# Linear attention of a two-block network: the next head's preparation in nine pieces in place of seven

## The chip, the cores and the metric

The kernel runs on one core of a Trainium2 chip. The metric is the device time of one execution, in microseconds (us); lower is better.

## The reference, cut to what matters

The program is a small network: two layers with four mixers each, then a block with gated linear attention, then a mixture of experts. Only the linear attention matters here. It has 4 heads; the keys of a head have 128 dimensions, its values 256. It runs over 512 tokens and 256 context tokens in chunks of 64, forwards and backwards:

```python
def step(s, inp):                      # one chunk of 64 tokens
    qc, kc, vc, gc = inp
    cum = jnp.cumsum(gc, axis=2)
    last = cum[:, :, -1:, :]
    s_new = jnp.exp(last[:, :, 0, :])[..., None] * s + jnp.einsum(
        'bhjd,bhje->bhde', kc * jnp.exp(last - cum), vc)
    ...
    scores = jnp.einsum('bhid,bhjd,bhijd->bhij', qc, kc, decay)
    o = jnp.einsum('bhid,bhde->bhie', qc * jnp.exp(cum), s) + jnp.einsum(
        'bhij,bhje->bhie', scores, vc)
    return s_new, o
```

where `gc` is `log_sigmoid` of the gates, divided by 16. So each head needs the running sums of its log gates within each chunk, their exponentials on keys and queries, and then a chain of states from chunk to chunk.

## The kernel before, in words

The stage is `gla_heads`. For each head there are two streams of work, written as Python generators, one for each engine: `gla_prepare_stream` makes a head's operands, `gla_scan_stream` uses them. A `yield` ends a piece. `run` takes a plan, a list of stream numbers, and issues the next piece of the named stream on each engine. All engines follow the same plan, each with its own pieces, so the plan and the places of the `yield`s are each engine's program order. An engine works strictly in that order; semaphores hold it where data or a buffer is missing.

The plan first lists the whole preparation of head 0. Then, for heads 0 to 2, it mixes the 17 pieces of the scan of head h with the pieces of the preparation of head h+1 by `alternate(17, steps)`, which puts a piece in as soon as its share of the scan's pieces is done. The last head is scanned with no preparation beside it. A third stream (modulation, L1687 and L1694) puts one piece behind the first of each scan.

**The scan's 17 pieces.** Scores (L2816 on TensorE, masked by VectorE at L2896, and the first pair of update matmuls); values (L2833); then twelve steps s0 to s11, s0 to s3 over the context and s4 to s11 over the tokens. In step s TensorE makes the pair of update matmuls for step s+1 (L2803, one for each direction, into banks that alternate), and from s4 on multiplies the state of step s-1 into the output (L2849). VectorE adds the update to the decayed state (L2910, a pair; L2907 in s0). It may not overwrite a state buffer until the product that reads it is done. Three closing pieces: ScalarE squares the output (L2874); TensorE sums over a head (L2859) and ScalarE makes the root (L2877, L2879); VectorE reads the output out (L2918, L2919).

**The preparation's pieces.** TensorE makes the gates for z = 0 and z = 1, one direction each (L2554); ScalarE takes them (L2563, L2565) and makes the softplus (L2571, L2573). VectorE waits for it and makes the minimum (L2578) and three running sums (L2580), then the centring: totals, halves, two subtractions, an addition and a clamp (L2588 to L2594). Each of these waits for the one ahead of it. The values are turned (L2639) and copied (L2692, L2697). ScalarE makes the exponentials (L2598 to L2603) from the clamped sums, VectorE scales keys and queries with them (L2611, L2615, L2620, L2622), and last the keys are turned and copied (L2714).

The first head's gates are prepared in the projection stage ahead (`gla_project`), in the shadow of its matmuls, by the same helpers.

Of the kernel before, what the change touches and what calls it, by code (L numbers as in the profile page):

```python
# [28 lines left out]
ALU = mybir.AluOpType  # L29
AXX = mybir.AxisListType.X  # L30

P = 128
# [9 lines left out]
CH = 64  # L42
# [2235 lines left out]
class Gla:  # L2278
# [3 lines left out]
    LAT, SEG = S, S + CTX  # L2282
# [38 lines left out]
def gla_project(c, w, gates, ahead, sums, first_sums, swept):  # L2321
# [23 lines left out]
    with nc.Block() as block:  # L2345
# [140 lines left out]
        @block.vector  # L2486
        def _(dve):
            eng = nc.vector
            apply.dve(dve)
            dve.wait_ge(ctx["summed"], 1)  # L2490
            eng.tensor_tensor(c.ctxmod[:, :], c.ps[:, 7, 0:2 * KT], c.ctxmod[:, :], ALU.add).then_inc(ctx["ready"], 1)
            dve.wait_ge(ctx["ready"], 1)
            eng.tensor_scalar(ctx_gain, ctx_scale, 1.0, None, ALU.add).then_inc(ctx["ready"], 1)
            dve.wait_ge(ctx["ready"], 2)
            eng.tensor_tensor(ctx_gain, ctx_gain, c.cols2[:, C2_AT["norm1_g"]:C2_AT["norm1_g"] + KT], ALU.mult
                              ).then_inc(ctx["ready"], 1)
            dve.wait_ge(ctx["ready"], 3)

            def low(t):
                dve.wait_ge(ctx["high"], t + 1)  # L2500
                eng.scalar_tensor_tensor(c.ctx_lo[:, t, :], w.ctx_h[:, t, :], ctx_shift[:, t:t + 1],
                                         c.ctx_hi[:, t, :].bitcast(F32), ALU.add, ALU.subtract).then_inc(ctx["low"], 1)

            for t in range(n1):
                if t + 2 < n1:
                    qr.split_low(dve, (t + 2) % RING, (t + 2) // RING)
                if t == 5:
                    dve.wait_ge(ctx["rooted"], 2)
                if 5 <= t < 9:
                    for kt in range(2 * t - 10, 2 * t - 8):  # L2510
                        eng.scalar_tensor_tensor(w.ctx_h[:, kt, :], w.ctx_x[:, kt, :], ctx_gain[:, kt:kt + 1], ctx_rs,
                                                 ALU.mult, ALU.mult).then_inc(ctx["scaled"], 1)
                        if kt:
                            low(kt - 1)
                if t == 9:
                    low(KT - 1)
                    dve.wait_ge(low_split, 1)
                    eng.tensor_tensor(low_lo[:, :], low_w, low_hi[:, :].bitcast(F32), ALU.subtract).then_inc(low_split, 1)
                for n in early(t):
                    sums.add(dve, n)  # L2520

            def copy_ctx(s, g):
                dve.wait_ge(kv.multiplied, g * RING + s + 1)
                t = g * RING + s
                eng.tensor_copy(ctx_kv[:, t * CTX:(t + 1) * CTX], c.ps[:, RING + t % 2, 0:CTX]).then_inc(ctx_emptied, 1)
                if t < FIRST_GATE:
                    for n in late(t):
                        sums.add(dve, n)
                elif t == FIRST_GATE + 2:
                    gates.scan(dve, 0)  # L2530
                elif t == FIRST_GATE + 3:
                    gates.centre(0)
                elif t == FIRST_GATE + 5:
                    gates.scale(dve, 0)

            kv.split_first(dve, kv.split_low)
            kv.tiles(dve, kv.split_low, copy_ctx)


class GlaGates:  # L2540
# [31 lines left out]
        act.wait_ge(self.pr["exp"], h + 1)  # L2572
        self.c.nc.scalar.activation(cum, cum, ACT.Ln, bias=1.0).then_inc(self.pr["soft"], 1)  # L2573

    def scan(self, dve, h):
        eng, g, cum = self.c.nc.vector, self.w.g[h], self.w.cum[h]
        dve.wait_ge(self.pr["soft"], h + 1)
        self.chain(eng.scalar_tensor_tensor(g, g, 0.0, cum, ALU.min, ALU.subtract))  # L2578
        for i in range(3):
            self.chain(eng.tensor_tensor_scan(cum[:, i * S:(i + 1) * S], self.c.const("scan"), g[:, i * S:(i + 1) * S], 0.0,  # L2580
                                              ALU.mult, ALU.add))

    def centre(self, h):
        eng, w, g, cum, chain = self.c.nc.vector, self.w, self.w.g[h], self.w.cum[h], self.chain
        SEG = w.SEG
        chunks = lambda t: t.rearrange("p (c n) -> p c n", n=CH)
        bc = lambda t, n: t.unsqueeze(2).to_broadcast([P, n, CH])
        chain(eng.tensor_copy(w.tot, chunks(cum)[:, :, CH - 1]))  # L2588
        chain(eng.tensor_scalar(w.half, w.tot, 0.5, None, ALU.mult))
        f, r = cum[:, 0:SEG], cum[:, SEG:2 * SEG]  # L2590
        chain(eng.tensor_tensor(chunks(f), chunks(f), bc(w.half[:, 0:12], 12), ALU.subtract))
        chain(eng.tensor_tensor(r, g[:, SEG:2 * SEG], r, ALU.subtract))
        chain(eng.tensor_tensor(chunks(r), chunks(r), bc(w.half[:, 12:24], 12), ALU.add))
        eng.tensor_scalar(cum, cum, 80.0 * 16, -80.0 * 16, ALU.min, ALU.max).then_inc(self.pr["gate"], 1)  # L2594
# [31 lines left out]
def gla_prepare_stream(c, w, gates, pr, sn, copied):  # L2626
# [7 lines left out]
    def pe():  # L2634
        eng = nc.tensor

        def turn(bank, blocks):
            for n, x in enumerate(blocks):
                last = eng.transpose(bank[:, n * P:(n + 1) * P], x, c.const("ident"))  # L2639
            return last  # L2640

        for h in range(GLA_H):
            if h:
                eng.wait_ge(pr["k_out"], 6 * h)
                eng.wait_ge(copied, h)
                if h == 1:
                    eng.wait_ge(pr["v_out"], 4)
                gates.gate(eng, h, 0, A, B)
            yield
            if h:  # L2650
                eng.wait_ge(pr["z_in"], 8 * h + 4)
                gates.gate(eng, h, 1, A, B)
            yield
            if h:
                eng.wait_ge(pr["z_in"], 8 * h + 8)
            for j in range(2):
                v = c.p[:, w.v + 2 * h + j, :]
                turn(v_banks(h)[j], [v[:, n * P:(n + 1) * P] for n in range(4)]).then_inc(pr["v_turn"], 1)
            yield
            if h:  # L2660
                eng.wait_ge(pr["v_out"], 4 * h + 1)
            turn(v_banks(h)[2], [w.vc[:, 2 * h + j, n * P:(n + 1) * P] for j in range(2) for n in range(2)]
                 ).then_inc(pr["v_turn"], 1)
            yield
            yield
            yield
            if h:
                eng.wait_ge(pr["v_out"], 4 * h + 4)
            for i in range(3):
                eng.wait_ge(pr["k_done"], 4 * h + (1, 3, 4)[i])  # L2670
                if h and i == 2:
                    eng.wait_ge(pr["k_out"], 6 * h + 2)
                turn(k_banks(h)[i], [w.e_neg[:, n * P:(n + 1) * P] for n in range(4 * i, 4 * i + 4)]
                     ).then_inc(pr["k_turn"], 1)
            yield

    def act():
        eng, on = nc.scalar, nc.scalar.activation
        for h in range(GLA_H):
# [10 lines left out]
            for j in range(2):  # L2690
                eng.wait_ge(pr["v_turn"], 3 * h + j + 1)
                on(w.v_tok[q][:, 0:4, j * P:(j + 1) * P], v_banks(h)[j].rearrange("p (b n) -> p b n", n=P), ACT.Copy  # L2692
                   ).then_inc(pr["v_out"], 1)
            yield
            eng.wait_ge(pr["v_turn"], 3 * h + 3)
            for j in range(2):
                on(w.v_tok[q][:, 4:6, j * P:(j + 1) * P],  # L2697
                   v_banks(h)[2][:, 2 * j * P:2 * (j + 1) * P].rearrange("p (b n) -> p b n", n=P), ACT.Copy
                   ).then_inc(pr["v_out"], 1)
            yield  # L2700
            if h:
                eng.wait_ge(pr["gate"], h + 1)
# [14 lines left out]
    def dve():  # L2717
        eng = nc.vector
        for h in range(GLA_H):
            yield  # L2720
            yield
            if h:
                gates.scan(eng, h)
            yield
            if h:
                gates.centre(h)
            yield
            yield
            if h:
                gates.scale(eng, h, (lambda: eng.wait_ge(sn["e_scaled"], 2 * (h - 1))) if h >= 2 else None)  # L2730
            yield
            yield

    return dict(pe=pe, act=act, dve=dve, steps=7)


def gla_scan_stream(c, w, pr, sn, fill, filled, w_out):
# [245 lines left out]
def gla_heads(c, w, gates, pr, sums, fill, filled, w_out, swept):  # L2983
# [3 lines left out]
                                            "ms", "rs", "ended")}  # L2987
    mod = ModRows(c, "b2_mod", sums, lambda j: sums.sums[0][1][j][:, 0:S], lambda j: c.ps[:, 0, :], c.ps[:, 0, :])
    prep = gla_prepare_stream(c, w, gates, pr, sn, mod.copied)
    scan = gla_scan_stream(c, w, pr, sn, fill, filled, w_out)  # L2990

# [19 lines left out]
    modulation = dict(pe=sum_parts, dve=add_bias, act=copy_parts)  # L3011
    opened = open_gla_stream(c, w, gates, pr, sn, w_out, [(pr["k_out"], 6 * GLA_H), (sums.biased, 1), (mod.copied, sums.count)])
    streams = [scan, prep, modulation, opened]
    plan = [1] * prep["steps"]
    for h in range(GLA_H - 1):
# [893 lines left out]
```

## Time and profile before

| | us |
|---|---|
| median of 3 runs | 2521.93 (2519.75 to 2528.81) |
| the profiled execution, its own time | 2520.24 |
| its span | 2518.2 |
| TensorE busy | 2269.8 (90%) |
| VectorE busy | 1589.3 (63%) |
| ScalarE busy | 1075.6 (43%) |
| mean granted TensorE clock | 0.965 of full |

The span is the time from the first to the last instruction of the profiled execution; its own time has some 2 us more around it. Busy times are of the whole program. The stage `gla_heads` begins near 1927 us of the span and ends near 2092 us.

### The profile page before, as it was taken

The numbers are of one execution on the slowest core, as the hardware profiler recorded it, in microseconds if no ns is written. First come the engines' busy times: TensorE is split into PE (matmuls) and PEld (weight loads), VectorE is DVE, ScalarE is ACT, GpSimd is POOL, SyncE is SP. The second block draws the span as 40 slices with busy tenths as digits, with TensorE's granted clock in tenths as the row PEclk, the third lists the DMA queues.
The fourth block names the chain that finished last, engine by engine and source line by source line (L and its number), as shares of the span: only waits on it lengthen the run. The fifth ranks groups of instructions, "written<-read, shape, count | busy, mean of one in ns | idle before, by whom it ended". The sixth has DMA issues, their size and how long they took to land. (4 is left out here: it accounts for less than half of the span.)

```text
span 2518.2 us, 31929 instructions
## 1 busy us (share of the span) xinstructions
PE 2269.8 (90%) x11349; PEld 1814.9 (72%) x11349; DVE 1589.3 (63%) x2284; ACT 1075.6 (43%) x1628; POOL 123.3 (5%) x201
## 2 busy tenths in 40 slices
PE   4998689899999989877889999999999888699995
PEld 3776567678888867666667888788877676588884
DVE  6655656555567665665665555774633774699997
ACT  3343244443343235342343333423233443588884
POOL 0001100000000000110000000000000000011112
PEclk9999899999999999999999999998999999799997
DMA  7650000223225355200012223354633101699996
GB/s 293 210 185 9 1 34 1 83 77 97 94 76 210 118 178 201 65 1 1 35 43 81 95 92 103 137 172 162 223 109 134 34 1 43 264 401 412 413 411 233
DMA packets 95430, 348.29 MB, mean 138 GB/s; under 512 B 12360, under 2 KB 14520, under 8 KB 95056
## 3 DMA queue, kind: packets, MB, share of 16 engines
q1 hardware_dynamic: 88688, 323.67, 36.0%
q0 software_dynamic: 3888, 14.16, 1.5%
q10 hardware_dynamic: 2736, 8.92, 0.9%
q8 instruction: 70, 1.15, 0.2%
q14 instruction: 48, 0.39, 0.1%
HBM read 333.55 MB, written 21.54 MB: 141 GB/s over the span
## 5 line engine op out<-in xcount | busy, mean ns | idle before, releaser
L500 PE MATMUL ps<-a_hi,w_hi 128*128 128x512 f32 x1344 | 545.6, 406 | 28.8 <-DVE h_lo L406 18.1
L502 PE MATMUL ps<-a_hi,w_lo 128*128 128x512 f32 x1344 | 538.2, 400 | 0.0
L501 PE MATMUL ps<-h_lo,w_hi 128*128 128x512 f32 x1280 | 508.8, 398 | 0.0
L464 DVE TENSOR_TENSOR w_lo<-ring,w_hi 128x1024 fp32r<-128x1024 f32 x178 | 218.2, 1226 | 378.0 <-ACT w_hi L459 377.5
L459 ACT ACTIVATE w_hi<-ring 128x1024 fp32r<-128x1024 f32 x178 | 187.9, 1058 | 512.5 <-PE ps L502 507.1
L500 PEld LDWEIGHTS ps<-a_hi,w_hi 128*128 128x128 f32 x1344 | 255.9, 190 | 98.5 <-issue 26.8
L502 PEld LDWEIGHTS ps<-a_hi,w_lo 128*128 128x128 f32 x1344 | 255.8, 190 | 63.2
L501 PEld LDWEIGHTS ps<-h_lo,w_hi 128*128 128x128 f32 x1280 | 243.4, 190 | 60.7 <-issue 2.9
L3362 DVE TENSOR_TENSOR moe_w_lo<-p,moe_w_hi 128x1024 fp32r<-128x1024 f32 x204 | 240.2, 1222 | 8.0 <-ACT moe_w_hi L3461 2.0
L3461 ACT ACTIVATE moe_w_hi<-p 128x1024 fp32r<-128x1024 f32 x204 | 216.1, 1063 | 56.8 <-PE ps L3404 53.9
L2139 PE MATMUL ps<-p_lo,down_hi 128*128 128x512 f32 x352 | 138.0, 392 | 0.0
L3402 PE MATMUL ps<-moe_w_hi,moe_x_hi 128*128 128x512 f32 x272 | 108.9, 401 | 6.4 <-DVE moe_w_lo L3362 6.4
L3404 PE MATMUL ps<-moe_w_lo,moe_x_hi 128*128 128x512 f32 x272 | 107.2, 394 | 0.0
L3403 PE MATMUL ps<-moe_w_hi,moe_x_lo 128*128 128x512 f32 x272 | 106.9, 393 | 0.0
L2056 ACT ACTIVATE down_hi<-down_raw 128x1408 fp32r<-128x1408 f32 x32 | 44.2, 1380 | 144.7 <-PE ps L2140 144.7
L501 PE MATMUL ps<-y_lo,w_hi 128*128 128x512 f32 x192 | 76.6, 399 | 0.0
L2139 PEld LDWEIGHTS ps<-p_lo,down_hi 128*128 128x128 f32 x352 | 66.1, 188 | 14.3
L291 DVE SCALAR_TENSOR_TENSOR y<-vt,cond,y 128x1024 f32<-128x1024 f32 x56 | 70.7, 1280 | 5.7 <-DMA vt<-in_ada 5.7
L2060 DVE TENSOR_TENSOR down_lo<-down_raw,down_hi 128x1408 fp32r<-128x1408 f32 x32 | 52.0, 1625 | 33.7 <-ACT down_hi L2056 33.4
L1991 DVE SCALAR_TENSOR_TENSOR y<-ps,cols,y 128x510 f32<-128x510 f32 x88 | 65.9, 749 | 11.0 <-DVE y L1988 0.5
L1961 ACT ACTIVATE y<-ps,cols 128x512 f32<-128x512 f32 x88 | 67.3, 764 | 9.4 <-PE ps L502 9.4
L1988 DVE SCALAR_TENSOR_TENSOR y<-ps,cols,y 128x511 f32<-128x511 f32 x88 | 65.6, 746 | 4.6 <-ACT y L1961 4.6
(645 smaller groups left out, 4200.3 us busy)
## 6 DMA issues: line engine op xcount, KB each, us to landing
ring<-in_ffn_up SPq DMA_DIRECT2D x88, 512.0 KB, 3.4
ring<-in_w_in SPq DMA_DIRECT2D x72, 512.0 KB, 5.3
p<-in_moe_gate SPq DMA_DIRECT2D x68, 512.0 KB, 7.4
p<-in_moe_up SPq DMA_DIRECT2D x68, 512.0 KB, 7.4
p<-in_moe_down SPq DMA_DIRECT2D x68, 512.0 KB, 8.4
vt<-in_ada SPq DMA_DIRECT2D x64, 512.0 KB, 4.0
p<-in_ada SPq DMA_DIRECT2D x48, 512.0 KB, 5.4
down_raw<-in_ffn_down SPq DMA_DIRECT2D x32, 704.0 KB, 5.0
```

The source lines that it names most:

```text
L291: ins = nc.vector.scalar_tensor_tensor(out, self.piece[b], factor, out, ALU.mult, ALU.add)
L459: self.c.nc.scalar.activation(self.c.w_hi[:, s % 2, :], self.c.slot(s), ACT.Copy).then_inc(self.high, 1)
L464: self.c.nc.vector.tensor_tensor(self.c.w_lo[:, s % 2, :], self.c.slot(s), self.c.w_hi[:, s % 2, :].bitcast(F32), ALU.subtract).then_inc(s ...
L500: nc.tensor.matmul(bank, c.w_hi[:, s % 2, at], hi(kt), start=(kt == self.order[0]), stop=False)
L501: nc.tensor.matmul(bank, c.w_hi[:, s % 2, at], lo(kt), start=False, stop=False)
L502: return nc.tensor.matmul(bank, c.w_lo[:, s % 2, at], hi(kt), start=False, stop=(kt == self.order[-1]))
L2139: nc.tensor.matmul(bank, down.w_hi[n % 2][:, at], c.p_lo[:, kt, :], start=False, stop=False)
L3362: ops.tensor_tensor(m.w_lo[:, n % 4, :], m.raw[n], m.w_hi[:, n % 4, :].bitcast(F32), ALU.subtract).then_inc(low[n], 1)
L3402: nc.tensor.matmul(bank, x[0], w_hi, start=start, stop=False)
L3403: nc.tensor.matmul(bank, x[1], w_hi, start=False, stop=False)
L3404: return nc.tensor.matmul(bank, x[0], w_lo, start=False, stop=stop)
L3461: nc.scalar.activation(m.w_hi[:, n % 4, :], m.raw[n], ACT.Copy).then_inc(high[n], 1)
```

## The change

The preparation has nine pieces in place of seven, in each engine's generator. VectorE's running sums are cut in two pieces, one with the minimum and the first sum, one with the other two, and its centring likewise, after the forward subtraction. TensorE's and ScalarE's generators get two empty pieces each, so that their pieces keep their partners. By the larger number of pieces `alternate` also places all of them anew. In the projection the two halves of the centring are called one behind the other.

```diff
-    def scan(self, dve, h):
+    def running(self, dve, h, parts=(0, 1, 2)):
         eng, g, cum = self.c.nc.vector, self.w.g[h], self.w.cum[h]
-        dve.wait_ge(self.pr["soft"], h + 1)
-        self.chain(eng.scalar_tensor_tensor(g, g, 0.0, cum, ALU.min, ALU.subtract))
-        for i in range(3):
+        if 0 in parts:
+            dve.wait_ge(self.pr["soft"], h + 1)
+            self.chain(eng.scalar_tensor_tensor(g, g, 0.0, cum, ALU.min, ALU.subtract))
+        for i in parts:
             self.chain(eng.tensor_tensor_scan(...))
...
-    def centre(self, h):
+    def centre_first(self, h):
...
-        f, r = cum[:, 0:SEG], cum[:, SEG:2 * SEG]
+        f = cum[:, 0:SEG]
         chain(eng.tensor_tensor(chunks(f), chunks(f), bc(w.half[:, 0:12], 12), ALU.subtract))
+
+    def centre_second(self, h):
...
+        r = cum[:, SEG:2 * SEG]
         chain(eng.tensor_tensor(r, g[:, SEG:2 * SEG], r, ALU.subtract))
         chain(eng.tensor_tensor(chunks(r), chunks(r), bc(w.half[:, 12:24], 12), ALU.add))
         eng.tensor_scalar(cum, cum, 80.0 * 16, -80.0 * 16, ALU.min, ALU.max).then_inc(self.pr["gate"], 1)
...
@@ def pe():
             yield
+            yield
             if h:
                 eng.wait_ge(pr["v_out"], 4 * h + 1)
             turn(v_banks(h)[2], ...)
             yield
+            yield
...
@@ def act():
+            yield
             eng.wait_ge(pr["v_turn"], 3 * h + 3)
...
             yield
+            yield
             if h:
                 eng.wait_ge(pr["gate"], h + 1)
...
@@ def dve():
             if h:
-                gates.scan(eng, h)
+                gates.running(eng, h, (0,))
             yield
             if h:
-                gates.centre(h)
+                gates.running(eng, h, (1, 2))
+            yield
+            if h:
+                gates.centre_first(h)
+            yield
+            if h:
+                gates.centre_second(h)
             yield
...
-    return dict(pe=pe, act=act, dve=dve, steps=7)
+    return dict(pe=pe, act=act, dve=dve, steps=9)
```

## Rows read from the trace of the kernel before

**Rows 1.** The page, part 1: busy time, share of the span, instructions, by engine.

```profile
PE 2269.8 (90%) x11349; PEld 1814.9 (72%) x11349; DVE 1589.3 (63%) x2284; ACT 1075.6 (43%) x1628; POOL 123.3 (5%) x201
```

**Rows 2.** Timeline, VectorE, head 1's period: start, length, instruction, idle before.

```profile
...
1994.52 1.76 DVE L2578 SCALAR_TENSOR_TENSOR h<-h 128x1536 f32<-128x1536 f32 x1 [1.32 <-ACT h L2573]
1996.31 3.74 DVE L2580 TENSOR_TENSOR_SCAN h<-k,h 128x512 f32<-128x512 f32 x3
2000.09 1.66 DVE L2910 SCALAR_TENSOR_TENSOR h<-h,small,ps 128x256 f32<-128x256 f32 x4
2001.66 0.18 DVE L2588 COPY small<-h 128x24 f32<-128x24 f32 x1
...
2003.08 0.96 DVE L2592 TENSOR_TENSOR h<-h 128x768 f32<-128x768 f32 x1
...
2008.64 0.93 DVE L2910 SCALAR_TENSOR_TENSOR h<-h,small,ps 128x256 f32<-128x256 f32 x2 [0.83 <-PE ps L2849]
...
2014.95 0.75 DVE L2918 SCALAR_TENSOR_TENSOR w2b<-ps,cols,w2b 128x512 f32<-128x512 f32 x1 [2.07 <-ACT w2b L2879]
...
```

**Rows 3.** Timeline, TensorE, the same period.

```profile
...
1983.94 0.60 PE L2803 MATMUL ps<-w2b,p 128*128 128x256 f32 x2
...
1984.90 1.55 PE L2554 MATMUL ps<-vt,ring 16*128 16x512 f32 x4
...
1991.62 1.00 PE L2849 MATMUL ps<-w2b,h 128*128 128x64 f32 x8
1992.46 0.65 PE L2803 MATMUL ps<-w2b 128*128 128x256 f32 x2
...
1994.21 1.04 PE L2639 MATMUL ps<-k,p 128*128 128x128 f32 x8
...
2000.63 1.22 PE L2803 MATMUL ps<-w2b 128*128 128x256 f32 x2 [3.67 <-DVE h L2910]
...
2007.99 2.79 PE L2849 MATMUL ps<-w2b,h 128*128 128x64 f32 x24
...
```

**Rows 4.** Timeline, ScalarE, the same period.

```profile
...
1986.06 0.69 ACT L2563 ACTIVATE h<-ps,cols 128x512 f32<-128x512 f32 x1 [5.08 <-PE ps L2554]
...
1987.57 0.48 ACT L2565 ACTIVATE h<-ps,cols 128x256 f32<-128x256 f32 x1
...
2006.06 1.48 ACT L2598 ACTIVATE ring<-h 128x1536 f32<-128x1536 f32 x1 [0.21 <-DVE h L2594]
2007.45 1.13 ACT L2602 ACTIVATE ring<-h 128x512 f32<-128x512 f32 x2
2008.49 0.21 ACT L2603 ACTIVATE small<-small 128x24 f32<-128x24 f32 x1
2010.82 1.08 ACT L2874 ACTIVATE w2b<-ps 128x512 f32<-128x512 f32 x2 [2.12 <-PE ps L2849]
...
```

**Rows 5.** Timeline, VectorE's minimum and ScalarE's squares, heads 0 and 2.

```profile
...
1954.56 1.76 DVE L2578 SCALAR_TENSOR_TENSOR h<-h 128x1536 f32<-128x1536 f32 x1 [1.33 <-ACT h L2573]
...
1970.30 1.08 ACT L2874 ACTIVATE ring<-ps 128x512 f32<-128x512 f32 x2 [1.56 <-PE ps L2849]
...
2034.78 1.76 DVE L2578 SCALAR_TENSOR_TENSOR h<-h 128x1536 f32<-128x1536 f32 x1 [1.33 <-ACT h L2573]
...
2051.42 1.08 ACT L2874 ACTIVATE ring<-ps 128x512 f32<-128x512 f32 x2 [2.46 <-PE ps L2849]
...
```

**Rows 6.** Windows of 7 us behind TensorE's idle stretch, three heads.

```profile
core 0: us, PE busy (x) PEld busy (x) DVE busy (x) ACT busy (x) POOL busy (x), PEclk, DMA share, GB/s
1960.66:1967.66 7.00, 6.91 (x35) 6.24 (x35) 6.80 (x13) 2.22 (x4) 0.00 (x0) 0.76 0.00 1
2000.63:2007.63 7.00, 7.00 (x31) 6.37 (x32) 6.75 (x13) 2.23 (x4) 0.00 (x0) 0.63 0.00 0
2040.89:2047.89 7.00, 7.00 (x29) 6.35 (x30) 6.06 (x12) 2.22 (x4) 0.00 (x0) 0.58 0.00 0
```

**Rows 7.** Timeline, SyncE's DMA issues: the first load of expert weights.

```profile
...
2166.08 2.10 SPq L3376 DMA_DIRECT2D p<-in_moe_gate  x4
...
```

More of the change, by code:

```diff
@@ L2529, in copy_ctx @@
                 elif t == FIRST_GATE + 2:
-                    gates.scan(dve, 0)
+                    gates.running(dve, 0)
                 elif t == FIRST_GATE + 3:
-                    gates.centre(0)
+                    gates.centre_first(0)
+                    gates.centre_second(0)
                 elif t == FIRST_GATE + 5:
@@ L2589, in centre @@
         chain(eng.tensor_scalar(w.half, w.tot, 0.5, None, ALU.mult))
-        f, r = cum[:, 0:SEG], cum[:, SEG:2 * SEG]
+        f = cum[:, 0:SEG]
         chain(eng.tensor_tensor(chunks(f), chunks(f), bc(w.half[:, 0:12], 12), ALU.subtract))
+    def centre_second(self, h):
+        eng, w, g, cum, chain = self.c.nc.vector, self.w, self.w.g[h], self.w.cum[h], self.chain
+        SEG = w.SEG
+        chunks = lambda t: t.rearrange("p (c n) -> p c n", n=CH)
+        bc = lambda t, n: t.unsqueeze(2).to_broadcast([P, n, CH])
+        r = cum[:, SEG:2 * SEG]
         chain(eng.tensor_tensor(r, g[:, SEG:2 * SEG], r, ALU.subtract))
```

## The prediction

> **What bounds the kernel now.** I read the page first. TensorE is busy nearly throughout, but that is an average over stages, and the diff touches only three head periods of the linear attention [rows 1]. So I went to the timeline of one such period, head 1's scan with the preparation of head 2, engine by engine: VectorE [rows 2], TensorE [rows 3], ScalarE [rows 4]. In what follows s0 to s11 are the steps of the scan; each has an update on VectorE (pair of L2910), a pair of matmuls on TensorE that makes the next update (L2803), and from s4 on the products that add the state to the output (L2849). A pair has two halves, one for each direction.
>
> The period runs so. After the values (L2833) TensorE goes s0, gate z0 (L2554), s1, s2, gate z1, s3 and so on [rows 3]. ScalarE takes the gates and makes the softplus; VectorE waits for its end and starts the gate chain at 1994.52 [rows 2]. I call that moment X. The minimum (L2578) and three running sums (L2580) then hold VectorE without a break to 2000.09, and TensorE, which had run ahead, stands idle 3.67 us until s6's first half is there [rows 2, 3]. Then s6 and s7, all of the centring, s8, s9, and s10 at 2008.64. From 2000.63 TensorE works without a pause up to its last product, and the squares (L2874) start at 2010.82, just behind it [rows 3, 4]. So the end of the period is set by the softplus, 5.6 us of VectorE, and then TensorE's backlog. The exponentials (L2598 to L2603) began at 2006.06 and were done before the squares' data was: they cost nothing [rows 4]. Behind the squares the order is the same in both kernels: mean, root, readout at 2014.95 [rows 2], next head.
>
> What I count is therefore the distance from X to the squares. It is 15.74 us in head 0, 16.30 in head 1 and 16.64 in head 2 (from the start of L2578 to that of L2874; the other two heads are in [rows 5]). The three differ because TensorE's granted clock fell after the idle stretch: over the 7 us behind it the mean was 0.76, 0.63 and 0.58, with 0.5 the lower level, 1.2 GHz [rows 6]. Lost work time is 7 us by the missing share: 1.7, 2.6 and 2.9 us, together 7.2.
>
> **The change part by part.** Writing out the two plans (17 scan steps against 7 or 9 pieces, each piece put where its share of the scan is done):
>
> before: s0, G0, s1 s2, G1, s3 s4 s5, [minimum, 3 sums], s6 s7, [all centring], s8 s9 s10, exponentials;
> after: G0, s0 s1, G1, s2 s3, [minimum, sum 1], s4 s5, [sums 2 and 3], s6 s7, [centring, first], s8 s9, [centring, second], s10 s11, exponentials.
>
> The turn of the context values stays behind s7, scaling stays between s10 and the readout, the key turns stay last. No instruction, copy or DMA is added, and SP's and GpSimd's queues are not passed. In the projection the same instructions run in the same order, and for head 0 nothing runs beside the nine pieces: both cost 0.
>
> *The gates, one step earlier.* G1 now has one pair fewer ahead of it, and a pair takes 0.96 us (1983.94 to 1984.90) [rows 3]. The take of z0 begins 1.16 us behind G0 and lasts 2.0 us (1986.06 to 1988.05 [rows 4]), so it is out 3.15 us after G0's start. G1 must wait for that, and comes behind G0's 1.55 us and two pairs, 3.4 us after G0: no wait. X comes 0.93 us sooner. The updates s1 to s3 wait for the gates instead, but this is ahead of X: they are done 3 us before it.
>
> *VectorE behind X.* Minimum 1.79 us (to the next start), each sum 1.26, two steps together 1.57 (2000.09 to 2001.66), first centring 1.42 (2001.66 to 2003.08), second 2.94 to the clamp's end (2003.08 [rows 2] to the exponentials' start at 2006.06 [rows 4], less 0.04 from an end to what waits for it). Before, VectorE sat 1.3 us ahead of the minimum and had done s4 and s5 by then. Now it will sit some 3 us there, since s4 and s5 stand behind the minimum in its program: the split does not fill the wait, it lengthens it.
>
> *TensorE behind X.* Products of a step 0.84 us (1991.62 to 1992.46), the four context turns 0.44 (half of the eight value turns' 1.04, less the 0.16 by which the last matmul overlaps what follows, as in the products' row) [rows 3]. s4 starts at X+3.05, and TensorE resumes 0.54 behind it as it did at 2000.63: X+3.59. What it has ahead of the idle stretch is all it had before less two pairs and two products (3.6 us), so it falls idle near 1993.5 and resumes near 1997.2, for 3.7 us: the stretch moves and keeps its length. Then pair 6, products 5, pair 7, products 6: 3.6 us, X+7.2. Pair 8 needs s6, which starts at X+3.05+1.57+2.52 = X+7.14, hence X+7.68. Pair 8, products 7, turn, pair 9: 0.96+0.84+0.44+0.96 = 3.2, so products 8 start at X+10.88. s9 may not overwrite the state that products 8 read; before, s10 started 0.65 behind the products it waits for (2007.99 to 2008.64), so s9 starts at X+11.53 and lasts 0.87. VectorE alone would have been there at X+10.4 or so.
>
> *Centring, second, and the exponentials.* Clamp's end X+11.53+0.87+2.94 = X+15.34, exponentials 0.04 later. From their start to the next activation I take 2.54 us: 2006.06 to 2008.70, less the 0.1 by which an activation here starts ahead of its predecessor's end (2008.58 against 2008.49) [rows 4], and the squares stand behind them in ScalarE's program: X+17.92. s10 and products 11 are done by X+17, so the exponentials, formerly free, set the end. The scaling moves back too (to the end of its first exponential), but the readout's 2.07 us of waiting [rows 2] covers most of it and it moves with the squares.
>
> *Sum.* At full clock: 17.92-0.93 = 16.99 against 15.74, 16.30, 16.64: +1.25, +0.69, +0.35, together +2.3 us. If the clock falls as before, the loss L comes in ahead of products 8 and replaces the 0.48 us that pair 8 waited: 17.44+L-0.93, thus 18.21, 19.11, 19.41, or +2.5, +2.8, +2.8, together +8.1. The idle stretch that brought the fall has the same length (3.7 against 3.67), so I go near the upper case, with one stretch in some five getting off: **+7 us**. The last head has no preparation and moves along. Nothing absorbs it later: the first expert weights are asked for at 2166.08, behind the routing, and that comes from this stage's output [rows 7].
>
> The page Perfetto Trace Analysis of the Trainium skill, section Optimizing Scalar/DVE Operations, says that where VectorE and ScalarE are not saturated but cause bubbles on another engine, breaking up instructions may let work finish sooner. It speaks for this change; by it the bubbles would shrink, which is the first rival below.
>
> **Rivals.** *The idle stretch goes (faster).* VectorE's block of 5.6 us is cut to 3.05, 2.52, 1.42 and 2.94; if TensorE's idle time and the fall of the clock went with it, 3 x 3.67 + 7.2 = 18.2 us would go: 2521.9-18.2 = 2504. It decides if TensorE has work for more than X+3.59 in front of it. Against it: it has 3.6 us less in hand. A smaller form: if only the exponentials were clear of the squares, the squares would follow s10 (X+14.56+0.91+0.8-0.93 = 15.3), -0.4, -1.0, -1.3: -2.7, 2519. Against it: program order. Chance of a gain in either form 0.10, above 0.5% 0.02.
>
> *Nothing (the pieces hide).* If products 8 do not hold s9 and clock stays high, the clamp ends at X+14.64 and the squares start at X+17.22-0.93 = 16.3: +0.2 in all, 2522. For it: the margin that holds s9 is only about 1 us at full clock. With the full-clock case of +2.3 (2524): 0.25.
>
> *A second fall of the clock (slower still).* TensorE would have two more gaps in each head, about 1.4 us ahead of products 11 and 1.7 ahead of the mean. If the clock falls there, mean and score products run at half speed on the path: as much again as behind the first gap, 1.7 to 2.9 us a head, +7: 2536. The page TensorE: Matmul & The Clock Gate of the Trainium skill, Part 1, has it that the throttled clock is the resting state and activity lifts it; the trace agrees as far as [rows 6] go. Before, gaps of this size behind the squares (0.69 and 1.76 us) left the clock at full. Chance 0.10.
>
> **How the numbers follow.** Forecast +7: 0.55. Profiled execution 2520.2 us (span 2518.2) would become 2527; the median of the three runs is 1.7 above it, so 2521.9+7 = 2529. Range: from the hidden case less a little, 2520, to the second fall, 2536; this leaves out the large gain and ends beyond +14. A measurement of this kernel can't tell a change within 0.5%, 12.6 us, from none. Only the full gain (0.02) is faster by more; slower by more takes the second fall and more (0.06); the rest, 0.92, is within.
>
> **What the profile would show.** L2578 0.9 us earlier within each period, with some 3 us of idle VectorE ahead of it; TensorE's idle stretch still near 3.7 us but between products 4 and pair 6; an idle stretch of VectorE ahead of s9 released by L2849; the squares released by ScalarE's own exponentials, not by L2849, 17.9 to 20.3 us behind L2578; period 42 to 43 us in place of 40. I am wrong if pieces 4 and 5 leave TensorE no idle stretch, if s9 starts right behind s8, or if the clock behind the gap stays at full in all three heads.

## The result, and the profile after

The changed kernel takes 2536.6 us (median of 6 runs, 2533.6 to 2538.8) against 2521.3 (6 runs, 2519.8 to 2528.8): ratio 1.0058, 95% interval 1.0048 to 1.0068. That is 15.3 us more, where the forecast was 7 us more (2528.8), the range ended at 2536, and slower by more than 0.5% had a chance of 0.06. The direction was right, the size half.

VectorE in head 1's period, from the timeline of the changed kernel (start, length, instruction, idle before). It answers to [rows 2]; L2580 is the minimum, L2582 the sums, L2929 the updates, L2590 to L2603 the centring, L2937 the readout.

```profile
1998.27 1.76 DVE L2580 SCALAR_TENSOR_TENSOR h<-h 128x1536 f32<-128x1536 f32 x1 [3.08 <-ACT h L2574]
2000.07 1.23 DVE L2582 TENSOR_TENSOR_SCAN h<-k,h 128x512 f32<-128x512 f32 x1
2001.33 1.66 DVE L2929 SCALAR_TENSOR_TENSOR h<-h,small,ps 128x256 f32<-128x256 f32 x4
...
2007.64 0.93 DVE L2929 SCALAR_TENSOR_TENSOR h<-h,small,ps 128x256 f32<-128x256 f32 x2 [1.35 <-PE ps L2868]
...
2011.54 0.93 DVE L2929 SCALAR_TENSOR_TENSOR h<-h,small,ps 128x256 f32<-128x256 f32 x2 [0.77 <-PE ps L2868]
...
2014.37 0.96 DVE L2603 TENSOR_SCALAR h<-h 128x1536 f32<-128x1536 f32 x1
2015.24 0.87 DVE L2929 SCALAR_TENSOR_TENSOR h<-h,small,ps 128x256 f32<-128x256 f32 x2
...
2023.81 0.75 DVE L2937 SCALAR_TENSOR_TENSOR w2b<-ps,cols,w2b 128x512 f32<-128x512 f32 x1 [3.54 <-ACT w2b L2898]
```

TensorE in the same period, answering to [rows 3]; L2822 are the pairs, L2868 the products, L2878 the mean.

```profile
2001.87 1.22 PE L2822 MATMUL ps<-w2b 128*128 128x256 f32 x2 [3.76 <-DVE h L2929]
...
2010.89 1.00 PE L2868 MATMUL ps<-w2b,h 128*128 128x64 f32 x8
...
2012.65 1.89 PE L2868 MATMUL ps<-w2b,h 128*128 128x64 f32 x16
2015.77 1.10 PE L2868 MATMUL ps<-w2b,h 128*128 128x64 f32 x8 [1.23 <-DVE h L2929]
2018.53 3.78 PE L2878 MATMUL ps<-w2b,k 128*128 128x512 f32 x4 [1.65 <-ACT w2b L2893]
```

ScalarE, answering to [rows 4]: the exponentials (L2607 to L2612) and the squares (L2893).

```profile
2015.36 1.48 ACT L2607 ACTIVATE ring<-h 128x1536 f32<-128x1536 f32 x1 [4.47 <-DVE h L2603]
2016.75 1.13 ACT L2611 ACTIVATE ring<-h 128x512 f32<-128x512 f32 x2
2017.79 0.21 ACT L2612 ACTIVATE small<-small 128x24 f32<-128x24 f32 x1
2017.90 1.06 ACT L2893 ACTIVATE w2b<-ps 128x512 f32<-128x512 f32 x2
2022.35 0.69 ACT L2896 ACTIVATE w2b<-ps,k 128x512 f32<-128x512 f32 x1 [3.38 <-PE ps L2878]
```

The reader is to see three things. VectorE waits 3.08 us for the softplus, then 1.35 and 0.77 us for products of TensorE. The squares start 0.11 us behind the exponentials' last start, and have no wait on TensorE of their own: they are held by ScalarE's program order. And the mean, 1.98 us before, takes 3.78.

The last is the clock. Windows of 7 us in the changed kernel, first behind the first gap in each head (answering to [rows 6]), then around the mean:

```profile
core 0: us, PE busy (x) PEld busy (x) DVE busy (x) ACT busy (x) POOL busy (x), PEclk, DMA share, GB/s
1958.11:1965.11 7.00, 7.00 (x37) 6.39 (x38) 6.25 (x12) 0.00 (x0) 0.00 (x0) 0.76 0.00 0
2001.87:2008.87 7.00, 7.00 (x30) 6.24 (x31) 5.54 (x11) 0.00 (x0) 0.00 (x0) 0.65 0.00 0
2046.36:2053.36 7.00, 7.00 (x31) 6.25 (x31) 5.57 (x12) 0.00 (x0) 0.00 (x0) 0.65 0.01 2
1973.00:1980.00 7.00, 5.49 (x12) 2.91 (x12) 3.11 (x10) 3.56 (x8) 3.11 (x6) 0.53 0.00 0
2017.50:2024.50 7.00, 5.49 (x12) 2.91 (x12) 3.46 (x10) 3.56 (x8) 0.00 (x0) 0.54 0.00 0
2062.00:2069.00 7.00, 5.31 (x12) 2.90 (x12) 3.46 (x10) 3.56 (x9) 0.00 (x0) 0.55 0.00 0
```

The same stretch around the mean in the kernel before, head 1:

```profile
2010.50:2017.50 7.00, 4.56 (x47) 3.04 (x48) 4.83 (x12) 4.96 (x9) 0.00 (x0) 1.00 0.01 2
```

Behind the first gap the clock falls as it did before (0.76, 0.65, 0.65 against 0.76, 0.63, 0.58 in [rows 6]). Around the mean it is at the lower level, 1.2 GHz, in all three heads, where before it was at full.

Two measures serve all that follows. The first is the stage's length, from the copy of s0 in head 0 (L2907, now L2926) to the squares of the last head: 2081.36-1937.09 = 144.3 us before, 2094.34-1937.73 = 156.6 after, +12.3. What lies outside it differs by 3.8 us between the two profiled executions; among all the executions profiled below, the way from the last squares to the first load of expert weights took 84.1 to 86.4 us and the rest 352.0 to 354.6, whatever the change, so I do not count that as the change's. The stage itself began (copy of s0 in head 0) between 1934.4 and 1938.4 us in all of them but two. In runs 10 and 11 it began at 1946.7 and 1945.4: their profiled executions, 2528.9 and 2541.5 us, were the slowest of their runs, and what made them so lies for the most part ahead of the stage. Each version's stage is read from one execution. The second measure is the distance from the minimum's start to the squares and to the readout in heads 0, 1, 2.

### The profile page after: what moved, and what is told of

The parts are those of the page before. It is cut to its first block and busy times, and to the rows that moved or that the text cites. A ratio compares the mean times of both kernels' runs of the same rounds, so it can differ in the third digit from the quotient of the medians.

```text
span 2534.3 us, 31932 instructions
## 1 busy us (share of the span) xinstructions
PE 2282.2 (90%) x11349; PEld 1820.7 (72%) x11349; DVE 1588.2 (63%) x2284; ACT 1074.7 (42%) x1628; POOL 124.3 (5%) x201
```

## The experiments

All twelve runs use the changed kernel's nine pieces with a plan written out: `places` gives for each piece the scan piece (0 to 16; s0 is 2, s11 is 13) behind which it stands. The new places are 1, 3, 5, 7, 9, 11, 13, 15, 16; the old, in the same pieces, 2, 4, 7, 7, 9, 9, 12, 14, 16. The pieces in order: gate z0, gate z1, minimum with first sum, other sums, first half of the centring (and the context values), second half, exponentials, scaling, key turns.

```diff
+    places = [...]
     plan = [1] * prep["steps"]
     for h in range(GLA_H - 1):
-        steps = alternate(scan["steps"], prep["steps"])
-        at = steps.index(0) + 1
-        plan += steps[:at] + [2] + steps[at:]
+        for i in range(scan["steps"]):
+            plan += [0] + [2] * (i == 0) + [1] * places.count(i)
```

| run | median us | ratio, 95% | stage us | squares behind minimum | mean |
|---|---|---|---|---|---|
| before | 2521.3 | | 144.3 | 15.74, 16.30, 16.64 | 1.98, 1.99, 1.98 |
| changed | 2536.6 | 1.0048 to 1.0068 | 156.6 | 18.88, 19.63, 19.86 | 3.78, 3.78, 3.78 |
| 1 old places | 2520.5 | 0.9992 to 1.0009 | 144.2 | 15.74, 16.28, 16.63 | 1.98, 1.98, 1.98 |
| 2 gates early | 2520.2 | 0.9985 to 1.0003 | 142.8 | 15.73, 16.99, 15.75 | 1.98, 1.98, 1.98 |
| 3 sums split | 2531.7 | 1.0028 to 1.0054 | 155.2 | 18.06, 18.83, 19.60 | 1.98, 1.98, 3.66 |
| 4 centring split | 2534.7 | 1.0035 to 1.0061 | 157.0 | 17.88, 18.87, 19.05 | 3.78, 3.78, 3.78 |
| 5 exponentials behind | 2533.1 | 1.0045 to 1.0074 | 157.4 | 17.89, 19.04, 19.62 | 3.78, 3.63, 3.63 |
| 6 later gaps filled | 2531.6 | 1.0028 to 1.0054 | 154.6 | 19.50, 19.71, 20.77 | 1.98, 1.98, 1.98 |
| 7 all gaps filled | 2523.4 | 1.0006 to 1.0025 | 147.8 | 17.80, 17.80, 18.09 | 1.98, 1.98, 1.98 |
| 8 old, gap filled | 2524.2 | 1.0006 to 1.0024 | 147.4 | 15.74, 15.74, 18.07 | 1.98, 1.98, 3.78 |
| 9 s10 ahead | 2534.3 | 1.0030 to 1.0062 | 158.9 | 17.09, 17.71, 17.84 | 1.98, 1.98, 1.98 |
| 10 s8 between | 2518.3 | 0.9978 to 0.9996 | 142.7 | 16.55, 17.07, 15.45 | 1.98, 1.98, 1.98 |
| 11 gap at product filled | 2532.3 | 1.0025 to 1.0057 | 155.7 | 18.89, 21.36, 19.18 | 1.98, 3.46, 2.81 |
| 12 gap at mean filled | 2533.6 | 1.0032 to 1.0066 | 158.0 | 18.88, 19.79, 21.93 | 2.39, 2.77, 2.93 |

The last column is the length of the mean's four matmuls in the timeline of the profiled execution. Ratios are against runs of the kernel before on the same chip, whose medians were 2520.6 to 2521.5.

### 1: the pieces at the old places

```diff
+    places = [2, 4, 7, 7, 9, 9, 12, 14, 16]
```

> The changed kernel's nine pieces, each put where the same work stood in the seven-piece plan. Theory (places alone matter): every engine's order is that of before, so 2521 us, 0 within 3 us. Rival (the pieces themselves, more yields and calls, cost something): up to the full +15 us, 2536.

2520.5 us; the three distances are those of before to 0.02 us. More pieces cost nothing. The whole change is where they stand.

### 2: only the gates early

```diff
+    places = [1, 3, 7, 7, 9, 9, 12, 14, 16]
```

> Only the two gate pieces at the new places, all else at the old. Theory: the softplus ends 0.93 us sooner in each of three heads, VectorE's block and TensorE's resumption with it, the idle stretch shrinks from 3.67 to about 2.7 us: -2.8 us, 2518.4, and up to 4 us less if the granted clock then holds (2514). Rival (updates s1 to s3 come late behind the gates and delay the period): +1 to +3 us.

VectorE's wait for the softplus is 0.47 us in place of 1.32, TensorE's idle stretch 2.80 in place of 3.67: the 0.87 us is there (0.93 was reckoned). The stage is 1.5 us shorter, the median 1.1 us lower, and the interval of the ratio includes 1. The distance was 15.73 and 15.75 us in heads 0 and 2, a floor that run 8 explains, and 16.99 in head 1. And in head 0 the clock, which held behind the first gap, fell a little later, in front of head 1's scores (0.57 of full over the 4 us from 1976.68), behind a wait of TensorE of 2.02 us for the copies of the turned keys (L2727); before, 2.01 us of the same wait left it at full. So the gain is of the right kind and half the size, and too small to be shown by the runs alone.

### 3 and 4: one split each

```diff
+    places = [2, 4, 5, 7, 9, 9, 12, 14, 16]     # 3: sums split
+    places = [2, 4, 7, 7, 9, 11, 12, 14, 16]    # 4: centring split
```

> Only the running sums cut in two, with s4 and s5 between them, all else at the old places; the centring stays whole between s7 and s8. Theory: TensorE's idle stretch grows to about 4.7 us and pair 10 waits for s8 behind the centring; squares 17.2 to 17.9 us behind the minimum in place of 15.7 to 16.6: +3 to +5 us, 2524 to 2526. Rival (the sums' split is harmless, the centring's is all of it): 0.

> Only the centring cut in two, with s8 and s9 between, all else at the old places. Theory: s9 waits for products 8, so the second half and the exponentials come late and hold the squares: 16.4 us behind the minimum plus the clock's loss of 1.7 to 2.9, +7 us, 2529; with a second fall of the clock ahead of the mean (2.1 us a head more) 2535. Rival (squares still follow TensorE, exponentials are hidden): 0.

Each alone costs nearly all: +10.9 us of the stage for the sums, +12.7 for the centring; together, with the gates early, +12.3. They don't add, and they hold the period in different places. In 3 the squares never stood behind the exponentials: they waited 1.57 us for TensorE, and TensorE had waited 1.39 us ahead of pair 10 for s8, which stood behind the whole centring (head 1). In 4 the timeline of VectorE and of ScalarE shows the two holders that the prediction names, in head 1:

```profile
2011.48 0.93 DVE L2929 SCALAR_TENSOR_TENSOR h<-h,small,ps 128x256 f32<-128x256 f32 x2 [2.16 <-PE ps L2868]
...
2014.30 0.96 DVE L2603 TENSOR_SCALAR h<-h 128x1536 f32<-128x1536 f32 x1
```

```profile
2015.30 1.48 ACT L2607 ACTIVATE ring<-h 128x1536 f32<-128x1536 f32 x1 [5.00 <-DVE h L2603]
...
2017.84 1.06 ACT L2893 ACTIVATE w2b<-ps 128x512 f32<-128x512 f32 x2
```

s9 waits 2.16 us for products 8, and the second half of the centring, the clamp and the exponentials stand behind it. I had 16.4 us and the clock's loss of 1.7 to 2.9, so 18.1 to 19.3; it was 17.9 to 19.1. The second fall of the clock came in all three heads and made it the 2535 of the expectation. For 3 I had named +3 to +5 and it was +10.9: s7 waited for products 6 (1.37 us in head 1) ahead of the whole centring, which I had left out there, and the clock fell again in head 2's mean and in front of head 1's scores (0.57 over the 4 us from 1980.22).

### 5: the exponentials behind the squares

```diff
+    places = [1, 3, 5, 7, 9, 11, 14, 15, 16]
```

> The changed kernel with one piece moved: the exponentials stand behind the squares in ScalarE's order instead of ahead of them. Theory (exponentials hold the squares and open the gap in which the clock falls a second time): squares some 1.5 us closer to the minimum, mean at full clock, but the scaling now waits for the exponentials and holds the readout; 2 us a head back, 2530. Rival (TensorE's backlog holds the squares): 2536 or more, as the root comes later behind 2.5 us of exponentials.

ScalarE's timeline, head 1:

```profile
2016.30 1.09 ACT L2893 ACTIVATE w2b<-ps 128x512 f32<-128x512 f32 x2 [6.03 <-PE ps L2868]
2017.27 1.48 ACT L2607 ACTIVATE ring<-h 128x1536 f32<-128x1536 f32 x1
```

The squares now wait for TensorE (6.03 us), 1.0, 0.6 and 0.2 us sooner behind the minimum than in the changed kernel. So the exponentials' hold on the squares is real and small. The mean still took 3.63 us and more, though the gap ahead of it had shrunk from 1.65 to 0.69 us: my view that the exponentials open the gap in which the clock falls does not stand by itself. The 1.23 us gap ahead of the last product, which the second half of the centring makes by standing in front of s10, was still there. In head 0 the keys' copies then came late, TensorE waited 3.21 us for them, and the clock fell once more in front of head 1's scores. 2533.1 us lies between the two numbers, and the stage, 157.4, is no shorter than the changed kernel's.

### 6, 7 and 8: gaps filled with matmuls that nothing reads

```diff
+        def warm(n, bank=None):
+            for _ in range(n):
+                eng.matmul(c.ps[:, 7 if bank is None else bank, 2 * P:4 * P], c.const("ones"), c.k[:, 0:2 * P], start=True, stop=True)
...
+                    if s == STEPS - 1 and z == 0 and h < GLA_H - 1:   # 6 and 7, ahead of the last product
+                        warm(2)
...
+            if h < GLA_H - 1:                                        # 6 and 7, ahead of the mean
+                warm(3)
...
+                if s == 5 and h < GLA_H - 1:                         # 7; in 8: s == 7, warm(7, 1), old places
+                    eng.wait_ge(pr["v_out"], 4 * (h + 1) + 2)
+                    warm(5, 1)
```

> The changed kernel with idle-time matmuls that nothing reads, two ahead of the last product and three ahead of the mean in heads 0 to 2 (128x256 each, 0.48 us), so that TensorE's second and third gap are filled. Theory (the second fall of the clock costs 2.1 us a head): mean at 1.98 us instead of 3.78, -6 us against the changed kernel, 2530. Rival (the fall comes from elsewhere, or filling delays the work): 2536 or more.

> As the one before, and five such matmuls also in the first gap, ahead of pair 6. Theory: with no fall of the clock at all the changed order costs what the prediction's full-clock sum says, squares 17.9 us behind the minimum: 2521 + 2.3 + 0.5, near 2524. Rival (waits between VectorE and TensorE cost more than the clock): 2528 or more.

In 6 the mean is back at 1.98 us in all heads and the readout stands 4.1 to 4.5 us behind the squares, where it was 5.9 to 6.3; the median is 5.0 us lower than the changed kernel's. But the stage is only 2.0 us shorter, though the readouts give back 5.4: the squares came 1.6 us later in all, and in head 0 TensorE now waited 2.35 us for the keys' copies in place of 0.92 and the clock fell there instead, at 1978.1, so that head 1's minimum stood 1.4 us further behind the readout.

In 7 the clock holds at full behind the first gap and around the mean in all three heads. Windows of the run, behind the first gap and around the mean in heads 0 to 2:

```profile
1953.00:1960.00 7.00, 6.47 (x40) 5.43 (x39) 6.85 (x13) 0.00 (x0) 0.00 (x0) 1.00 0.05 19
1968.50:1975.50 7.00, 4.35 (x33) 2.57 (x33) 4.80 (x12) 4.82 (x10) 3.11 (x6) 1.00 0.00 1
2011.00:2018.00 7.00, 4.94 (x50) 3.07 (x49) 5.16 (x12) 5.28 (x11) 0.00 (x0) 1.00 0.00 0
2052.00:2059.00 7.00, 4.95 (x50) 3.15 (x49) 5.16 (x12) 5.28 (x11) 0.00 (x0) 1.00 0.01 2
```

It still fell once, as in run 6 in front of head 1's scores, behind the same 2.35 us:

```profile
1974.52 0.63 PE L2648 MATMUL ps<-k,ring 128*128 128x128 f32 x4 [2.35 <-ACT p L2727]
```

```profile
1976.00:1978.00 2.00, 1.79 (x17) 1.42 (x14) 1.19 (x4) 0.81 (x2) 1.14 (x2) 0.50 0.00 0
```

The squares come 17.80, 17.80 and 18.09 us behind the minimum: the prediction's full-clock chain gave 17.92. The stage is 3.5 us longer than before (2.3 by that chain; 1.2 is the longer way from head 0's readout to head 1's minimum, where the clock fell), the median 2523.4. So filling all three gaps takes 8.8 us off the stage's +12.3. That is not quite the clock's share of the difference, since the kernel before has the first fall too: by the floor of 15.74 us that run 8 shows, it cost the old order 0, 0.56 and 0.90 us.

> The old places with seven such matmuls in the 3.67 us gap ahead of pair 8, in heads 0 to 2. Theory: clock holds, squares 14.8 us behind the minimum in place of 15.7 to 16.6: -4.4 us, 2517. Rival (filling does not keep the clock up, or delays pair 8): 0 to +2.

In the old order the filling held the clock in heads 0 and 1, and the distance went to 15.74 and stopped there. TensorE's timeline shows why:

```profile
1995.97 3.24 PE L2816 MATMUL ps<-k 128*128 128x256 f32 x14
1999.81 0.70 PE L2826 MATMUL ps<-w2b 128*128 128x256 f32 x2 [0.59 <-DVE h L2936]
...
2005.65 0.70 PE L2826 MATMUL ps<-w2b 128*128 128x256 f32 x2 [1.73 <-DVE h L2936]
```

At full clock TensorE catches up and waits 1.73 us ahead of pair 10 for s8, which stands behind the whole centring. The floor of the old order is thus 15.7 us and not 14.8 as I had expected. In head 2 the clock fell all the same, at 2046.4, and stayed low through the mean (3.78 us), and the run was slower than before (interval 1.0006 to 1.0024). The gaps were the same in all three heads (0.59, 1.73, 0.69 us), so their lengths alone do not tell where it falls. Filling one gap is no safe gain.

### 9: s10 ahead of the second half, exponentials behind the squares

```diff
+    places = [1, 3, 5, 7, 9, 12, 14, 15, 16]
```

> The changed kernel with the second half of the centring behind s10, and the exponentials behind the squares. Theory (the gap ahead of the last product, made by the half centring in front of s10, brings the second fall of the clock): no such gap, mean at 1.98 us, squares 15.4 us plus the first fall's loss behind the minimum; the scaling then waits for the exponentials, so the readout stands some 22.6 us behind the minimum in place of 25.1 to 25.8: 2527. Rival (the second fall is a late consequence of the first gap): mean still 3.6 us or more, 2533.

With neither the gap ahead of the last product nor more than 0.69 us ahead of the mean, the mean ran at full clock in all heads, as the theory had it; so the fall around the mean comes from the gaps near it and is no late effect of the first. But the time did not follow: the readout stood 23.7 to 24.4 us behind the minimum, TensorE then waited 1.36 us for the scaled keys (L2620) and 1.25 to 4.52 us for the keys' copies (L2727), and the clock fell there instead, in front of the next head's scores and values (0.50 over the 4 us from the start of the scores, in all three heads). The stage was the longest of all, 158.9 us.

### 10: only s8 between the halves of the centring

```diff
+    places = [1, 3, 7, 7, 9, 10, 12, 14, 16]
```

> Gates early as in the second run; sums whole; centring cut, but only s8 between its halves, s9 and s10 behind. Theory: s9 finds products 8 done, pair 10 no longer waits for a whole centring, the second half ends about 12.3 us behind the minimum, exponentials hidden: squares 14.9 to 16.5 us behind it and the minimum 0.87 us sooner: 2516 to 2520. Rival (any cut of the centring costs): 2525 or more.

2518.3 us, ratio 0.9987 (0.9978 to 0.9996), stage 142.7 us. VectorE, head 2:

```profile
2051.51 0.96 DVE L2593 TENSOR_TENSOR h<-h,small 128x768 f32<-128x768 f32 x1
2052.51 0.48 DVE L2929 SCALAR_TENSOR_TENSOR h<-h,small,ps 128x256 f32<-128x256 f32 x1
2053.15 0.48 DVE L2929 SCALAR_TENSOR_TENSOR h<-h,small,ps 128x256 f32<-128x256 f32 x1 [0.16 <-PE ps L2868]
2053.55 0.95 DVE L2601 TENSOR_TENSOR h<-h 128x768 f32<-128x768 f32 x1
```

A cut of the centring costs little where the step put in finds its products all but done: the wait is 0.16 us here, and 0.61 and 0.26 us for the two halves in head 0; the stage, 142.7 us, is that of run 2 without the cut, 142.8. Where the clock's loss was short (head 2) the squares came 15.45 us behind the minimum, less than the old order's floor; in heads 0 and 1 it was longer and they came at 16.55 and 17.07. This is the only version whose interval lies below 1, by 0.04% to 0.22%. Its stage is no shorter than that of run 2, so the gain may be the gates' and not the cut's. The two medians, 2518.3 and 2520.2, each stand against their own of the kernel before (2521.5 and 2521.3).

### 11 and 12: one of the two later gaps filled

> The changed kernel with two idle-time matmuls ahead of the last product only. Theory (both gaps together bring the second fall): one filled gap is enough in most heads, mean 1.98 us, 2530 to 2532. Rival (the gap ahead of the mean alone brings it): mean 3.78 us, 2536.

> The changed kernel with three idle-time matmuls ahead of the mean only. Theory (both gaps together): mean 1.98 us in most heads, 2530 to 2532. Rival (the gap ahead of the last product alone brings it): clock already down when the filling starts, mean 3.78 us, 2536.

Run 11 has only the `warm(2)` of run 6, run 12 only the `warm(3)`. The means took 1.98, 3.46 and 2.81 us in 11, and 2.39, 2.77 and 2.93 in 12, between the 1.98 of both filled and the 3.78 of none. What they tell is when the clock fell. In 12 it was down from 1971.1 us on in head 0, as the last product ended and the filling began, in head 1 from 2015.5, while the filling ran, and in head 2 from 2059.8, in the gap ahead of the last product, which starts at 2060.11. In head 0:

```profile
1970.00:1971.00 1.00, 1.00 (x9) 1.00 (x10) 0.34 (x1) 1.00 (x2) 0.00 (x0) 1.00 0.00 0
1971.00:1972.00 1.00, 1.00 (x4) 0.82 (x4) 0.89 (x2) 1.00 (x3) 0.00 (x0) 0.54 0.00 0
```

So the gap ahead of the last product (1.22 to 1.52 us) brings the fall with no gap ahead of the mean: the rival was right on that. Its 3.78 us did not come, since the clock was back before the mean ended; the filling itself ran at the lower level (2.74 us for three matmuls in head 0), so the mean also started late. In 11 the gap ahead of the last product was down to 0.31 and 0.60 us in heads 1 and 2, and the clock fell at 2027.6 and 2071.9, during the mean, behind the gap of 1.65 us. In its head 0 the mean ran at full and the clock fell in front of the next scores, as in run 6. So each of the two gaps can bring the fall without the other, and my theory that it takes both does not stand. Filling only one is not enough; filling both (run 6) or leaving 0.69 us ahead of the mean and nothing ahead of the last product (run 9) kept the mean at full in all heads.

## Why the prediction was off

**Placing and the gates: right.** The two orders were written out correctly; run 1 shows that placing is all. The minimum moved 0.87 us forward against its gates by VectorE's waits in run 2, 0.93 reckoned; measured from the copy of s0 it is 0.7 to 1.2 us in the changed kernel.

**VectorE ahead of and behind the minimum: right.** It sits 3.08 us (some 3 predicted), and s4 comes 3.06 us behind the minimum's start (3.05).

**TensorE's first gap: right.** 3.76 us (3.7), at X+3.60 (3.59) in head 1, and the clock falls behind it as before.

**s9 held by products 8, second half and exponentials late: right, mechanism and price.** Predicted distances with the clock's fall 19.14, 20.04, 20.34; measured 18.88, 19.63, 19.86, 0.3 to 0.5 us under it. Without a fall 17.92 predicted, 17.80 measured (run 7). The sum of the three growths is 9.7 us less 2.8 for the earlier minimum: 6.9, and that is the +7 of the forecast. Two readings on the way were off without touching the sum. VectorE alone would have been at s9 at X+10.9 (7.14+1.57+1.42+0.79) and not X+10.4, so the margin that holds it is smaller: in run 7 s9 waits 0.43 us. And with the clock down s7 too waits, 1.35 us for products 6, which the prediction does not have.

**The chance of a second fall of the clock: the step that failed.** The sum puts it at nothing; the prediction has it as a rival with 0.10, "as much again as behind the first gap, 1.7 to 2.9 us a head, +7: 2536". It came in all three heads of the changed kernel: mean 3.78 us in place of 1.98, readout 6.3, 5.9 and 5.9 us behind the squares against 4.1, 5.7 us in all. A head's period was 43.8 and 44.5 us, where 42 to 43 was forecast. Filling the two gaps brought the mean back to 1.98 us and took 2.0 us off the stage (run 6); filling the first as well took 8.8 (run 7). What I set against it was that before, gaps of 0.69 and 1.76 us left the clock at full. That read each gap by itself. Ahead of those gaps, before, TensorE had worked from 2000.63 to 2010.78 without a pause; in the changed order a gap of 1.23 us stands 1.1 us in front of a gap of 1.65 us, with only the last product between. The prediction's own numbers (1.4 and 1.7 us) had both gaps. They do not make a rule: runs 11 and 12 have the fall behind either gap without the other, and in runs 3 and 8 gaps of 1.40 and 1.73 us, each followed by one of 0.69, left the clock at full up to the end of the mean in two heads and not in the third. Why it falls in one head and not in another stays open. With the second fall the sum is 6.9+5.7 = 12.6 us in the stage, against 12.3; the last 3 us of the median lie outside it and I can't tell them from chance.

**The rivals.** The idle stretch did not go: the page Perfetto Trace Analysis of the Trainium skill, section Optimizing Scalar/DVE Operations, is not borne out here, since breaking the block up moved TensorE's bubble (3.67 to 3.76 us) and made two more. Run 10 does not show the gain either, as its stage is that of run 2. The page TensorE: Matmul & The Clock Gate of the Trainium skill, Part 1, has the throttled clock as the resting state. The traces agree in the main: around the mean 1.00 with all gaps filled, 0.53 to 0.55 with them open. They also show a fall in head 2 of run 8, where the longest gap was 1.73 us.

**The range.** It ended at 2536, and the median, 2536.6, lies 0.6 us past it. It held the second fall at its middle price but nothing on top of it.

## What to carry to other kernels

Cutting a long block of an engine helps only if the steps put between the parts find their inputs ready. Here each of the two cuts let a chained step in that waits for another engine, and the rest of the block, with what the third engine makes of it, stood behind that wait. Before cutting, go down the program order of each engine and ask what the piece moved ahead waits for, and what was hidden only because the block was early. And count TensorE's short gaps as a risk and not as nothing: behind gaps of 1.2 to 1.7 us the clock fell in all three heads of the changed kernel, and a fall there cost 1.8 to 2.1 us a head at the readout, against 1.1 to 1.8 us at the squares for the fall behind the long gap (changed kernel against run 7). Filling them can move the fall instead of taking it away.

## What the runs showed of the hardware that was not expected

- The mean's matmuls took 1.98 us with the granted clock at 1.00 and 3.78 us with it near 0.5 around them (run 7 and the changed kernel), and 1.98 and 3.46 us in heads 0 and 1 of one execution (run 11). In the changed kernel the clock was low there behind two gaps of 1.2 to 1.5 and 1.6 to 1.7 us, and at full behind 0.69 us alone (before, and run 9). Either gap brought it without the other (runs 11 and 12).
- The same wait of some 2.0 us for the keys' copies in head 0 left the clock at full in the kernel before and in runs 1, 8 and 10, and was followed by a fall (0.57 over the next 4 us) in runs 2 and 3. So the length of the last gap does not settle it.
- Keeping TensorE busy is no guarantee: in run 8 the 3.67 us gap was filled in each head, and the clock fell in head 2 all the same, behind a gap of 1.73 us, for some 10 us. In run 7 all three gaps were filled, and it fell behind the next wait, of 2.35 us, in head 0.
- Seven 128x256 matmuls whose results nothing reads took 3.24 us (run 8) and kept the granted clock at 1.00 over the stretch behind them in heads 0 and 1.
